# A hybrid decoder step on one Trainium2 core: the squared sums of four norms as two split matmuls in place of one plain fp32 matmul

## The chip, the core and the metric

The kernel runs on one core of a Trainium2 chip (trn2). The metric is the device time of one launch in microseconds, as the median of several executions. The core has five engines with instruction streams of their own: TensorE (PE, matmuls), VectorE (DVE), ScalarE (ACT), GpSimd (POOL) and SyncE (SP, which here only issues DMAs). They wait for each other through semaphores.

## The reference

One decoder layer over 1024 prompt rows and 8 decode rows, all fp32. The parts that matter here are its norms: the LayerNorm behind the convolution, the norm of each head's retention output `o` (the out-norm), and the RMS norms of m and h.

```python
def rms_norm(x, w):
    xf = x.astype(jnp.float32)
    y = xf * lax.rsqrt(jnp.mean(xf * xf, axis=-1, keepdims=True) + EPS)
    return (y * w.astype(jnp.float32)).astype(x.dtype)
...
    a_out = jax.nn.silu(layer_norm(conv, conv_ln_w, conv_ln_b)) @ w_conv_out
...
    S_new, o = retention_scan(qf, kf, vf, ret_state.astype(jnp.float32))
    o = o * lax.rsqrt(jnp.mean(o * o, axis=-1, keepdims=True) + EPS)
    o = o.reshape(B, T, RET_V_WIDTH).astype(xn.dtype)
    b_out = (jax.nn.silu(g) * o) @ w_ret_out

    merged = jax.nn.sigmoid(gate_a) * a_out + jax.nn.sigmoid(gate_b) * b_out
    return merged @ w_o, new_buf, S_new
...
    m, new_buf, S_new = mixer(rms_norm(x, n_mix_pre), conv_buf, ret_state, pos, w_in, w_dw, b_dw,
                              conv_ln_w, conv_ln_b, w_conv_out, w_ret_out, w_o)
    h = x + rms_norm(m, n_mix_post)
    f = jnp.square(jax.nn.relu(rms_norm(h, n_ffn_pre) @ w_up)) @ w_down
    return h + rms_norm(f, n_ffn_post), new_buf, S_new
```

## The kernel before

All activations are held transposed: channels on the 128 partitions, the T = 1032 rows along the free dimension. So the sum over channels that a norm needs is a sum over partitions. VectorE first adds the squares of the channel tiles into one tile, and TensorE then multiplies it by an all-ones 128x128 matrix `ones`; each partition of the result holds the sum. That matmul is plain fp32.

All large products are fp32 by splitting: an operand is a high part (rounded to fp32r by a copy) and a low part (the fp32 value less the high part, again fp32r), and a product is three fp32r matmuls, high by high, high by low and low by high. ScalarE makes the high part of a weight tile, GpSimd the low part, in a ring of three places. Where matrices are large the kernel uses a scheme of seven products for a 2x2 block of tiles: the input projection is 20 units `v` of 7 steps `j`, written (v,j); a step is one product of 24 matmuls of 258 columns. Its results are evicted from PSUM by ScalarE and VectorE in fixed steps; an eviction named e6 or e5 (VectorE, after steps 4 and 5) frees a bank that TensorE needs at step 6, or at step 0 of the next unit. The FFN has 14 up and 16 down units of the same kind.

Between the steps of a unit stands other work, by a schedule written out by hand: after product (v,j) each engine's code calls its `unit_turn(v, j)`, and tables give the turn `x = 7 (v - 13) + j` (and `y = 7 (v - 9) + j`) at which a part is placed. The norms are placed by `NORM_SQUARE` (ScalarE squares 2x344 elements), `NORM_SUM` (VectorE adds the halves), `NORM_STAT` (TensorE's sum, and the root of it on ScalarE: Ln, then Exp) and `NORM_SCALE` (VectorE multiplies, `head_norm`). ScalarE comes to turn j when product j is done; VectorE runs its turns 1 to 4 between the evictions of steps 1 and 4.

The sums by `ones` are:
- three of the first norm at the start (`x_stat`, 344 columns) and the last norm (`f_ones`)
- four of LayerNorm (`ln_stat`, 2x258 columns), for mean and variance of each half of the rows
- twelve of the out-norm (`out_stat`, 344 columns): six of head pair 0 in units 15 to 19, six of head pair 1 (p = 1) in the groups of 36 matmuls behind the units (`b_part`, the first product by `w_ret_out`), after sub-tiles 3, 5, 7, 9, 12 and 14 (`turns_`)
- three of the norm after `w_o` (`mix_stat`, 344 columns)
- two of h (`h_stat`, 2x258 columns) in up unit 9

In pair 1 VectorE also multiplies the finished groups by their gate (`product_gate(e)`), whose end releases on GpSimd an addition `product_add(e)`, and it works the decode rows of the retention.

Of the kernel before, what the change touches and what calls it, by code (L numbers as in the profile page):

```python
# [27 lines left out]
P = 128  # L28
# [26 lines left out]
HT = T // 2  # L55
# [35 lines left out]
X_RET = 13  # L91
RET_A = {1: 0, 3: 1, 6: 2, 8: 3, 11: 4, 13: 5, 16: 6, 18: 7}
# [27 lines left out]
def build(nc, xT, wseq, vecs, wdwT, cacheT, s_in, rope, mask_d, ident_d,  # L120
# [8 lines left out]
    with ExitStack() as ctx:  # L129
# [95 lines left out]
        ones, _ = place("ones", [P, P])  # L225
        vec, _ = place("vec", [P, NVEC])
# [51 lines left out]
        hist_ld = sem("hist_ld")  # L278
# [35 lines left out]
        xs_sc = sem("xs_sc")  # L314
        xs_sum = sem("xs_sum")
        xs_hi = sem("xs_hi")
        xs_lo = sem("xs_lo")
        xw_hi = sem("xw_hi")
        xw_lo = sem("xw_lo")
# [29 lines left out]
        on_ad = sem("on_ad")  # L349
        on_st = sem("on_st")  # L350
# [62 lines left out]
        R_X, R_LN, R_ON, R_M, R_F = 0, CHUNKS, CHUNKS + 2, CHUNKS + 14, 2 * CHUNKS + 14  # L413
        E_WOB = done(S_WOB - 1)
# [185 lines left out]
        def _(sp):  # L600
# [11 lines left out]
            sp.dma_start(hist[:], cacheT).then_inc(hist_ld, 16)  # L612
# [4 lines left out]
            def unit_weights(v):  # L617
# [16 lines left out]
                sp.wait_ge(xw_lo, STEPS * (v - 1) + 6)  # L634
# [124 lines left out]
            for v in range(NV):  # L759
                d = v - UPV  # L760
                p, g = d % 4, d // 4
                if v + 1 < NV:
                    n = OFF + S_FAST + 4 * (v + 1)
                    sp.wait_ge(s_op, 4 * v + 3)
                    sp.wait_ge(q_lo, STEPS * v + 1)
                    sp.dma_start(raw[:, 0, :], wseq[n]).then_inc(raw_ld[0], 16)
                    sp.wait_ge(s_op, 4 * v + 4)
                    sp.wait_ge(q_lo, STEPS * v + 2)
                    sp.dma_start(raw[:, 1, :], wseq[n + 1]).then_inc(raw_ld[1], 16)
                    sp.wait_ge(q_lo, STEPS * v + 4)  # L770
                    sp.dma_start(raw[:, 2, :], wseq[n + 2]).then_inc(raw_ld[2], 16)
                    sp.wait_ge(q_lo, STEPS * v + 5)
# [66 lines left out]
        def _(pool):  # L839
# [85 lines left out]
            def unit_low(v, k):  # L925
# [4 lines left out]
                pool.wait_ge(xw_hi, q + 1)  # L930
                pool.tensor_tensor(lo, src, hi.bitcast(F32), ALU.subtract).then_inc(xw_lo, 1)  # L931
# [58 lines left out]
            def low(v, i):  # L990
# [4 lines left out]
                pool.wait_ge(q_hi, q + 1)  # L995
                pool.tensor_tensor(lo, src, hi.bitcast(F32), ALU.subtract).then_inc(q_lo, 1)  # L996
# [18 lines left out]
        def _(pe):  # L1015
# [208 lines left out]
            def unit_product(v, k):  # L1224
# [18 lines left out]
            def unit_turn(v, j):  # L1243
# [124 lines left out]
            def mix_stat(c):  # L1368

                pe.wait_ge(wo_sum, 6 + 4 * (c + 1))  # L1370
# [4 lines left out]
                pe.matmul(ps[:, 6 + c % 2, 0:CH], ones[:], gbuf[:, 3, c * CH:(c + 1) * CH],  # L1375
                          start=True, stop=True).then_inc(m_st, 1)
# [79 lines left out]
            def product(v, i, between=None):  # L1456
# [67 lines left out]
        def _(act):  # L1524
# [53 lines left out]
            def x_gain(k):  # L1578

                act.activation(x_in[:, k, :], x_in[:, k, :], ACT.Copy, scale=vec[:, V_PRE + k:V_PRE + k + 1]  # L1580
                               ).then_inc(xs_sc, 1)

            def x_operand_hi(i):

                if i == 5:
                    act.wait_ge(mm, done(15))
                    act.activation(xn_h[:, 0:QK, HALVES[1]], sx_5[:], ACT.Copy).then_inc(xs_hi, 1)
# [5 lines left out]
                act.activation(sx_h[:, i - 2], src, ACT.Copy).then_inc(xs_hi, 1)  # L1593
# [41 lines left out]
            def unit_high(v, k):  # L1635
# [14 lines left out]
                act.activation(XRINGS[q % RING][0], src, ACT.Copy).then_inc(xw_hi, 1)  # L1650
# [1503 lines left out]
```

## Time and profile before

| | us |
|---|---|
| median of 3 runs | 1497.67 |
| lowest and highest | 1497.33, 1498.96 |
| span of the profiled execution, first to last instruction | 1495.6 |
| TensorE matmuls busy | 1475.2 (99%) |
| VectorE, GpSimd, ScalarE busy | 1001.0, 842.0, 635.4 |

The profile is of one execution. Its span is 2.1 us below the median of the runs. TensorE's granted clock is 2.4 GHz throughout (0.997 of full speed in the mean). In the rows below, a row of a timeline is: start, duration, engine, line, operation, output <- inputs, shape, count, and in brackets the idle time before it and who ended it. Matmuls are pipelined, and the duration of one covers its way through the array, so that rows overlap; consecutive matmuls of one kind and line are merged (x2, x4).

### The profile page before, as it was taken

To read this page: it belongs to the slowest core of one execution; us is meant where nothing else is said; L and a number is where in the kernel's file an instruction comes from. 1 tells how busy PE (TensorE), PEld (TensorE's weight loads), DVE (VectorE), ACT (ScalarE), POOL (GpSimd) and SP (SyncE) were. 2 spreads that over 40 slices of the span, in tenths; PEclk is the share of its full clock that TensorE was granted. 3 is DMA by queue.
4 is the path that set the end of the run, shared out by engine and by line. 5 is a ranking of instruction groups with operands and counts; after the bars stand their busy time and mean duration, and the time that the engine had idled before them with its cause. 6 is when DMAs were issued, how large, how long until landed. Compare 5 with 4: busy or idle time off the path is not lost.

```text
span 1495.6 us, 28307 instructions
## 1 busy us (share of the span) xinstructions
PE 1475.2 (99%) x11336; PEld 1455.2 (97%) x11336; DVE 1001.0 (67%) x1251; ACT 635.4 (42%) x929; POOL 842.0 (56%) x571
## 2 busy tenths in 40 slices
PE   8999999999999999999999999999999999999996
PEld 5999999999999999999999999999999999999995
DVE  7999888856545724576715876766657765574847
ACT  5533444344544541131213855556556332332333
POOL 3377776777545653257565445555555655554555
PEclk9999999999999999999999999999999999999998
DMA  6013333322356258621421144566759575454634
GB/s 217 22 42 94 114 114 113 113 80 65 112 176 205 75 200 296 219 80 50 149 78 50 29 149 171 199 237 219 253 193 326 203 285 189 142 208 156 227 107 170
DMA packets 110091, 229.13 MB, mean 153 GB/s; under 512 B 8960, under 2 KB 20992, under 8 KB 108304
## 3 DMA queue, kind: packets, MB, share of 16 engines
q1 hardware_dynamic: 95296, 204.30, 39.7%
q10 hardware_dynamic: 14672, 23.09, 4.6%
q8 instruction: 89, 1.46, 0.4%
q14 instruction: 34, 0.28, 0.1%
HBM read 154.41 MB, written 72.95 MB: 152 GB/s over the span
## 4 chain that ended last, share of the span: by engine, by line
PE 96%; POOL 1%; DMA 1%; ACT 1%; issue 1%; DVE 0%; POOLq 0%; SPq 0%; DVEq 0%; ACTq 0%
PE ps L1476 40%; PE ps L1237 26%; PE ps L1026 16%; PE ps L1402 3%; PE ps L1389 3%; PE ps L1074 2%; PE ps L1164 1%; PE ps L1169 1%; PE ps L1180 1%; PE ps L1166 1%; DMA cva_h<-conv_scratch 1%; PE ps L1147 0%; PE ps L1152 0%; PE ps L1194 0%; POOL w_l L931 0%
## 5 line engine op out<-in xcount | busy, mean ns | idle before, releaser
L1476 PE MATMUL ps<-tx_h,w_h 128*128 128x258 f32 x960 | 271.5, 283 | 0.0
L1476 PE MATMUL ps<-tx_l,w_h 128*128 128x258 f32 x960 | 271.3, 283 | 0.0
L1476 PE MATMUL ps<-tx_h,w_l 128*128 128x258 f32 x960 | 271.1, 282 | 0.0
L996 POOL TENSOR_TENSOR w_l<-raw,w_h 128x512 fp32r<-128x512 f32 x120 | 185.6, 1551 | 147.6 <-ACT w_h L2033 147.1
L1476 PE MATMUL ps<-fx_l,w_h 128*128 128x258 f32 x720 | 203.7, 283 | 0.0
L1476 PE MATMUL ps<-fx_h,w_h 128*128 128x258 f32 x720 | 203.6, 283 | 0.0
L1476 PE MATMUL ps<-fx_h,w_l 128*128 128x258 f32 x720 | 203.4, 282 | 0.0
L1476 PEld LDWEIGHTS ps<-tx_h,w_h 128*128 128x128 f32 x960 | 181.4, 189 | 0.1
L1476 PEld LDWEIGHTS ps<-tx_l,w_h 128*128 128x128 f32 x960 | 181.4, 189 | 0.1
L1476 PEld LDWEIGHTS ps<-tx_h,w_l 128*128 128x128 f32 x960 | 181.2, 189 | 0.0
L2328 DVE SCALAR_TENSOR_TENSOR ps<-u_ext,wdw,ps 128x512 f32<-128x512 f32 x232 | 155.2, 749 | 0.0
L2033 ACT ACTIVATE w_h<-raw 128x512 fp32r<-128x512 f32 x120 | 75.7, 631 | 186.8 <-PE ps L1476 179.7
L996 POOL TENSOR_TENSOR w_l<-sum_y,w_h 128x512 fp32r<-128x512 f32 x60 | 91.9, 1532 | 110.2 <-ACT w_h L2033 110.2
L1476 PEld LDWEIGHTS ps<-fx_h,w_h 128*128 128x128 f32 x720 | 136.2, 189 | 0.0
L1476 PEld LDWEIGHTS ps<-fx_l,w_h 128*128 128x128 f32 x720 | 136.0, 189 | 0.0
L1476 PEld LDWEIGHTS ps<-fx_h,w_l 128*128 128x128 f32 x720 | 135.9, 189 | 0.0
L1237 PE MATMUL ps<-xn_h,w_h 128*128 128x258 f32 x416 | 119.6, 287 | 0.0
L1237 PE MATMUL ps<-xn_l,w_h 128*128 128x258 f32 x416 | 117.5, 282 | 0.0
L1237 PE MATMUL ps<-xn_h,w_l 128*128 128x258 f32 x416 | 117.4, 282 | 0.0
L2884 DVE TENSOR_TENSOR fac<-ps,fac 128x516 f32<-128x516 f32 x79 | 54.6, 691 | 83.3 <-PE ps L1476 83.3
L931 POOL TENSOR_TENSOR w_l<-raw,w_h 128x512 fp32r<-128x512 f32 x54 | 76.6, 1418 | 55.2 <-ACT w_h L1650 55.1
L850 POOL TENSOR_TENSOR w_h<-raw,zero 128x512 fp32r<-128x512 f32 x36 | 42.0, 1167 | 108.8 <-PE ps L1026 50.2
(386 smaller groups left out, 4305.4 us busy)
## 6 DMA issues: line engine op xcount, KB each, us to landing
raw<-wseq_dram SPq DMA_DIRECT2D x260, 256.0 KB, 3.1
quad_scratch<-quad_h SPq DMA_DIRECT2D x16, 774.0 KB, 3.5
tx_h<-quad_scratch SPq DMA_DIRECT2D x12, 1032.0 KB, 10.4
tx_l<-hidden_scratch SPq DMA_DIRECT2D x12, 1032.0 KB, 12.8
gate_scratch<-gst SPq DMA_DIRECT2D x10, 1032.0 KB, 5.0
hidden_scratch<-hq_g SPq DMA_DIRECT2D x8, 1032.0 KB, 7.0
hidden_scratch<-stg_b SPq DMA_DIRECT2D x6, 1032.0 KB, 6.9
hq_g<-hidden_scratch SPq DMA_DIRECT2D x6, 1032.0 KB, 13.1
```

Of the source, the lines that this page charges most:

```text
L850: pool.tensor_tensor(hi, raw[:, s, :], zero[:, 0:1].broadcast_to([P, SLOT]), ALU.add).then_inc(w_hi, 1)
L931: pool.tensor_tensor(lo, src, hi.bitcast(F32), ALU.subtract).then_inc(xw_lo, 1)
L996: pool.tensor_tensor(lo, src, hi.bitcast(F32), ALU.subtract).then_inc(q_lo, 1)
L1026: out = pe.matmul(pch(g, c), w[a][:, place_, sub * P:(sub + 1) * P], xs[b][:, k, c * CH:(c + 1) * CH], start=(first and n == 0), stop=(las ...
L1074: out = pe.matmul(pch(G_U + t, c), wp[:, 2 * half + t, sub * P:(sub + 1) * P], x_in[:, k, c * CH:(c + 1) * CH], start=(k == 0), stop=(k == ...
L1237: out = pe.matmul(ps[:, 2 * n + s, 0:HC], XRINGS[q % RING][wa][:, kk * P:(kk + 1) * P], x_operand(i, xb, kk, s), start=(i < 3 and kk == 0 ...
L1389: out = pe.matmul(pch(g, m), (wo_h, wo_l)[a][:, slot, sub * P:(sub + 1) * P], MG[b][:, k, c * CH:(c + 1) * CH], start=(k == 0 and n == 0), ...
L1402: out = pe.matmul(pch(g, c), DIRECT_W[slot][a][:, (k % SLOT_TILES) * P:(k % SLOT_TILES + 1) * P], FX[b][:, k, c * CH:(c + 1) * CH], start= ...
L1476: out = pe.matmul(ps[:, 2 * n + s, 0:HC], RINGS[q % RING][wa][:, kk * P:(kk + 1) * P], OPS[x][xb][:, QK * kh + kk, at_:at_ + HC], start=(i ...
L2033: act.activation(RINGS[q % RING][0], src, ACT.Copy).then_inc(q_hi, 1)
L2328: out = dve.scalar_tensor_tensor(dst, u_, w_, bank, ALU.mult, ALU.add)
L2884: dve.tensor_tensor(dst, pair(n), dst, ALU.add).then_inc(ev_d, 1)
```

## The change

Twenty sums change; the other edits give semaphores of like use one name (`xw_hi` and `q_hi` become `sw_hi`, and so on), which moves nothing. `ones_r` is `ones` rounded to fp32r. For LayerNorm, out-norm, h and the first two chunks of the mix norm, ScalarE copies the sum tile into a high part, VectorE subtracts it for a low part, and TensorE multiplies both by `ones_r`, added in PSUM. In the diff `norm_high` and `ln_high` are ScalarE's copies, `square_low` and `ln_low` VectorE's subtractions. Some of the turns are moved by one, and `h_stat` goes from up unit 9 to 10.

```diff
-NORM_SQUARE = {20: 0, 24: 1, 28: 2, 32: 3, 39: 4, 42: 5}
-NORM_SUM = {21: 0, 26: 1, 30: 2, 33: 3, 40: 4, 43: 5}
-NORM_STAT = {23: 0, 27: 1, 31: 2, 34: 3, 41: 4, 44: 5}
-NORM_SCALE = {26: 0, 29: 1, 33: 2, 35: 3, 42: 4, 45: 5}
+NORM_SQUARE = {20: 0, 24: 1, 28: 2, 32: 3, 39: 4, 43: 5}
+NORM_SUM = {21: 0, 25: 1, 29: 2, 33: 3, 40: 4, 44: 5}
+NORM_SPLIT = {22: 0, 26: 1, 30: 2, 34: 3, 41: 4, 45: 5}
+NORM_STAT = {23: 0, 27: 1, 31: 2, 35: 3, 42: 4, 46: 5}
+NORM_SCALE = {26: 0, 29: 1, 33: 2, 36: 3, 43: 4, 47: 5}
...
-                    out = pe.matmul(ps[:, 6 + s, 0:HC], ones[:], u_ext[:, 0, at_:at_ + HC], start=True, stop=True)
+                    pe.matmul(ps[:, 6 + s, 0:HC], ones_r[:], u_hi_[:, at_:at_ + HC], start=True, stop=False)
+                    out = pe.matmul(ps[:, 6 + s, 0:HC], ones_r[:], u_lo_[:, at_:at_ + HC], start=False, stop=True)
...
-                pe.wait_ge(on_ad, 6 * p + i + 1)
+                pe.wait_ge(st_lo, S_ON + 6 * p + i + 1)
...
-                pe.matmul(ps[:, 6 + i % 2, 0:CH], ones[:], osq[p * (i % 2)][:, 0:CH],
-                          start=True, stop=True).then_inc(on_st, 1)
+                pe.matmul(ps[:, 6 + i % 2, 0:CH], ones_r[:], osq_h[p * (i % 2)][:], start=True, stop=False)
+                pe.matmul(ps[:, 6 + i % 2, 0:CH], ones_r[:], osq_l[p * (i % 2)][:], start=False, stop=True
+                          ).then_inc(on_st, 1)
...
-                if y == 4:
+                if y == 5:
                     taps_done()
-                    pe.wait_ge(ln_sum, 3)
+                    pe.wait_ge(one_r, 1)
+                    pe.wait_ge(st_lo, S_LN + 1)
                     ln_stat(0)
...
-                if y == 18:
+                if y == 19:
                     pe.wait_ge(ln_xc, 8)
-                    pe.wait_ge(ln_sum, 6)
+                    pe.wait_ge(st_lo, S_LN + 2)
                     ln_stat(0)
-                if y == 22:
+                if y == 23:
...
+            def norm_high(p, i):
+
+                b = p * (i % 2)
+                act.wait_ge(on_ad, 6 * p + i + 1)
+                act.activation(osq_h[b][:], osq[b][:, 0:CH], ACT.Copy).then_inc(st_hi, 1)
...
+            def square_low(p, i):
+
+                b = p * (i % 2)
+                dve.wait_ge(st_hi, S_ON + 6 * p + i + 1)
+                dve.tensor_tensor(osq_l[b][:], osq[b][:, 0:CH], osq_h[b][:].bitcast(F32), ALU.subtract
+                                  ).then_inc(st_lo, 1)
...
+                if y in (3, 18):
+                    ln_low(y // 18)
...
             norm_square(1, 1)
+            norm_high(1, 0)
+            norm_high(1, 1)
             for i in range(2 * CHUNKS):
                 norm_root(1, i)
...
                 if i + 2 < 2 * CHUNKS:
                     norm_square(1, i + 2)
+                    norm_high(1, i + 2)
...
             wob_out(0, 1)
+            mix_high(0)
...
             wob_out(1, 1)
+            mix_high(1)
...
-                    if v == 9 and i in (2, 5):
+                    if v == 10 and i in (2, 5):
                         h_stat(i // 3)
```

VectorE's stream of pair 1, from the first two adds to the gate of group 1. Before (L2505 is the add of the squares, L2512 `head_norm`, L2637 `product_gate`, L2500 the copy of a decode output):

```order
L2505 TENSOR_TENSOR osq_144<-osq_144 128x344
L2505 TENSOR_TENSOR osq_145<-osq_145 128x344
L2512 TENSOR_TENSOR v_95<-v_95,ps 128x2x344
L2484 COPY qd_b<-qk_94 128x2
...
L2505 TENSOR_TENSOR osq_144<-osq_144 128x344
L2500 COPY v_95<-ps 128x4
L2637 TENSOR_TENSOR bop_b<-ps,gb 128x1032
L2512 TENSOR_TENSOR v_95<-v_95,ps 128x2x344
L2505 TENSOR_TENSOR osq_145<-osq_145 128x344
L2512 TENSOR_TENSOR v_95<-v_95,ps 128x2x344
L2500 COPY v_95<-ps 128x4
L2637 TENSOR_TENSOR bop_b<-ps,gb 128x1032
```

The same stream in the changed kernel (L2564 the add, L2571 the new low part, L2578 `head_norm`, L2707 `product_gate`):

```order
L2564 TENSOR_TENSOR osq_155<-osq_155 128x344
L2564 TENSOR_TENSOR osq_156<-osq_156 128x344
L2571 TENSOR_TENSOR osq_l_151<-osq_155,osq_h_153 128x344
L2571 TENSOR_TENSOR osq_l_152<-osq_156,osq_h_154 128x344
L2578 TENSOR_TENSOR v_95<-v_95,ps 128x2x344
...
L2707 TENSOR_TENSOR bop_b<-ps,gb 128x1032
L2571 TENSOR_TENSOR osq_l_151<-osq_155,osq_h_153 128x344
L2578 TENSOR_TENSOR v_95<-v_95,ps 128x2x344
L2564 TENSOR_TENSOR osq_156<-osq_156 128x344
L2578 TENSOR_TENSOR v_95<-v_95,ps 128x2x344
L2571 TENSOR_TENSOR osq_l_152<-osq_156,osq_h_154 128x344
```

Low part 0 stands behind add 1, low part 2 behind the gate, and low part 3 behind `head_norm` 2.

ScalarE's stream at the same place in the changed kernel (L1775 Square, L1782 the new high part, L1547 and L1549 the root); before, it was the same without the rows of L1782:

```order
L1775 ACTIVATE osq_156<-v_95 128x688
L1782 ACTIVATE osq_h_153<-osq_155 128x344
L1782 ACTIVATE osq_h_154<-osq_156 128x344
L1547 ACTIVATE ps<-ps,eps_b 128x344
L1549 ACTIVATE ps<-ps 128x344
L1757 DMA rets_dram<-s_dec 128x2x256
L1775 ACTIVATE osq_155<-v_95 128x688
L1782 ACTIVATE osq_h_153<-osq_155 128x344
L1547 ACTIVATE ps<-ps,eps_b 128x344
L1549 ACTIVATE ps<-ps 128x344
L1775 ACTIVATE osq_156<-v_95 128x688
L1782 ACTIVATE osq_h_154<-osq_156 128x344
```

High part 0 stands behind Square 1, and each later root behind the high part of the sum after it.

VectorE around step 5 of unit 16 in the changed kernel (L2675 the eviction of step 4, L2571 the low part of sum 1 of pair 0, L2578 `head_norm`, L2680 the eviction of step 5); before, the add stood at the place of the low part:

```order
L2564 TENSOR_TENSOR osq_155<-osq_155 128x344
L2675 TENSOR_TENSOR v_95<-ps,v_95 128x516
L2571 TENSOR_TENSOR osq_l_151<-osq_155,osq_h_153 128x344
L2559 COPY v_105<-ps 128x4
L2578 TENSOR_TENSOR v_105<-v_105,ps 128x2x344
L2680 TENSOR_TENSOR v_95<-ps,v_95 128x516
```

The add went one turn ahead, and the low part came in front of `head_norm` and the eviction.

## Rows read from the trace of the kernel before

**Rows 1.** The page: span, and busy time of each engine.

```profile
span 1495.6 us, 28307 instructions
PE 1475.2 (99%) x11336; PEld 1455.2 (97%) x11336; DVE 1001.0 (67%) x1251; ACT 635.4 (42%) x929; POOL 842.0 (56%) x571
```

**Rows 2.** Waits of TensorE, the longest: us in total, times, longest.

```profile
PE ps L1074 <- DVE wp L2286: 5.8, 1, 5.8
```

**Rows 3.** Instructions that read `ones`, the out-norm: durations in ns, first and last start.

```profile
L1194 PE MATMUL ps<-osq,ones x24: 450/452/455, 477.0 to 662.1; 128*128 128x344 f32 x24
```

**Rows 4.** Timeline of TensorE around a mix sum and a LayerNorm sum.

```profile
800.41 0.32 PE L1389 MATMUL ps<-mg_h,wo_l 128*128 128x344 f32 x1
800.57 0.74 PE L1375 MATMUL ps<-gbuf,ones 128*128 128x344 f32 x2
...
801.30 0.32 PE L1389 MATMUL ps<-mg_l,wo_h 128*128 128x344 f32 x1
...
302.94 0.28 PE L1237 MATMUL ps<-xn_h,wx_l 128*128 128x258 f32 x1
303.06 1.03 PE L1131 MATMUL ps<-u_ext,ones 128*128 128x258 f32 x4
...
304.05 0.28 PE L1237 MATMUL ps<-sx_l,w_h 128*128 128x258 f32 x1
```

**Rows 5.** Timeline of TensorE, the out-norm sums 0, 2, 3, 4 and 5 of pair 1.

```profile
641.61 0.74 PE L1194 MATMUL ps<-osq,ones 128*128 128x344 f32 x2
...
649.30 0.74 PE L1194 MATMUL ps<-osq,ones 128*128 128x344 f32 x2
...
653.59 0.74 PE L1194 MATMUL ps<-osq,ones 128*128 128x344 f32 x2
...
658.41 0.74 PE L1194 MATMUL ps<-osq,ones 128*128 128x344 f32 x2
...
661.82 0.74 PE L1194 MATMUL ps<-osq,ones 128*128 128x344 f32 x2
```

**Rows 6.** Timeline of ScalarE at pair 1: Square 1, Ln of root 0, Square 2.

```profile
641.74 0.78 ACT L1750 ACTIVATE osq<-v 128x688 f32<-128x688 f32 x1 [3.60 <-issue]
642.42 0.50 ACT L1527 ACTIVATE ps<-ps,eps_b 128x344 f32<-128x344 f32 x1
...
647.66 0.78 ACT L1750 ACTIVATE osq<-v 128x688 f32<-128x688 f32 x1 [4.27 <-DVE s_dec L2494]
```

**Rows 7.** Timeline of VectorE at pair 1: add 1, gate 0, `head_norm` 1, add 3.

```profile
642.54 0.52 DVE L2505 TENSOR_TENSOR osq<-osq 128x344 f32<-128x344 f32 x1 [2.29 <-ACT osq L1750]
...
648.98 1.22 DVE L2637 TENSOR_TENSOR bop_b<-ps,gb 128x1032 f32<-128x1032 f32 x1
650.12 0.86 DVE L2512 TENSOR_TENSOR v<-v,ps 128x688 f32<-128x688 f32 x1
650.90 2.17 DVE L2505 TENSOR_TENSOR osq<-osq 128x344 f32<-128x344 f32 x1
```

**Rows 8.** Timeline of GpSimd at pair 1: `product_add(0)`.

```profile
650.28 2.41 POOL L951 TENSOR_TENSOR ma<-ma,bop_b 128x1032 f32<-128x1032 f32 x1 [4.59 <-DVE bop_b L2637]
```

**Rows 9.** Timelines of ScalarE, VectorE, GpSimd and TensorE at LayerNorm sum 2.

```profile
340.63 1.06 ACT L1670 ACTIVATE u_ext<-conv 128x1032 f32<-128x1032 f32 x1
...
346.28 0.67 ACT L1527 ACTIVATE ps<-ps,eps_b 128x516 f32<-128x516 f32 x1
...
345.41 0.70 DVE L2605 TENSOR_TENSOR v<-ps,v 128x516 f32<-128x516 f32 x1 [1.52 <-PE ps L1237]
...
346.45 1.29 POOL L931 TENSOR_TENSOR w_l<-raw,w_h 128x512 fp32r<-128x512 f32 x1
...
345.21 1.03 PE L1131 MATMUL ps<-u_ext,ones 128*128 128x258 f32 x4
```

**Rows 10.** Timelines of VectorE and GpSimd after product (16,5).

```profile
487.38 0.70 DVE L2610 TENSOR_TENSOR v<-ps,v 128x516 f32<-128x516 f32 x1 [1.54 <-PE ps L1237]
...
488.09 1.74 POOL L931 TENSOR_TENSOR w_l<-raw,w_h 128x512 fp32r<-128x512 f32 x1 [0.70 <-ACT w_h L1650]
```

More of the change, by code:

```diff
@@ L225, in build @@
         ones, _ = place("ones", [P, P])
+        ones_r, _ = place("ones_r", [P, P], F32R)
         vec, _ = place("vec", [P, NVEC])
@@ L244, in build @@
         sum_y, _ = place("sum_y", [P, SLOT], F32, a_ST + 4 * SLOT)
+        hms_h, _ = place("hms_h", [P, T], F32R, a_C0 + 8 * T)
+        hms_l, _ = place("hms_l", [P, T], F32R, a_ST + 8 * SLOT)
+        mst_h, _ = place("mst_h", [P, 2, CH], F32R, a_G)
+        mst_l, _ = place("mst_l", [P, 2, CH], F32R, a_G + 12 * T)
         hms, _ = place("hms", [P, T], F32, a_ST + 8 * SLOT)
@@ L248, in build @@
         rtab = [place(f"rtab{c}", [P, 2, HC], F32, a_Q + (8 * HC + 16) * c if c < 3 else a_PB)[0] for c in range(4)]
+        u_lo_, _ = place("u_lo_", [P, T], F32R, a_C1)
+        u_hi_, _ = place("u_hi_", [P, T], F32R, a_C1 + 4 * UW + 8)
+        osq_l = [place(f"osq_l{i}", [P, CH], F32R, (a_KT, a_PB)[i])[0] for i in range(2)]
+        osq_h = [place(f"osq_h{i}", [P, CH], F32R, (a_KT, a_PB)[i] + 4 * CH)[0] for i in range(2)]
         osq = [place("osq0", [P, 2 * CH], F32, a_KT)[0], place("osq1", [P, 2 * CH], F32, a_PB)[0]]
@@ L313, in build @@
         cvl_st = sem("cvl_st")
-        xs_sc = sem("xs_sc")
+        g_sc = sem("g_sc")
         xs_sum = sem("xs_sum")
[L316 to L319, printed above, removed]
+        op_hi = sem("op_hi")
+        op_lo = sem("op_lo")
+        sw_hi = sem("sw_hi")
+        sw_lo = sem("sw_lo")
         xw_op = sem("xw_op")
@@ L349, in build @@
         on_ad = sem("on_ad")
+        st_hi = sem("st_hi")
+        st_lo = sem("st_lo")
+        one_r = sem("one_r")
         on_st = sem("on_st")
@@ L1368, in mix_stat @@
             def mix_stat(c):
-                pe.wait_ge(wo_sum, 6 + 4 * (c + 1))
+                if c < 2:
+                    pe.wait_ge(st_lo, S_M + c + 1)
+                else:
+                    pe.wait_ge(wo_sum, 6 + 4 * (c + 1))
                 if c == 0:
@@ L1374, in mix_stat @@
                     pe.wait_ge(m_sc, 2)
-                pe.matmul(ps[:, 6 + c % 2, 0:CH], ones[:], gbuf[:, 3, c * CH:(c + 1) * CH],
-                          start=True, stop=True).then_inc(m_st, 1)
+                out = ps[:, 6 + c % 2, 0:CH]
+                if c < 2:
+                    pe.matmul(out, ones_r[:], mst_h[:, c, :], start=True, stop=False)
+                    pe.matmul(out, ones_r[:], mst_l[:, c, :], start=False, stop=True).then_inc(m_st, 1)
+                else:
+                    pe.matmul(out, ones[:], gbuf[:, 3, c * CH:(c + 1) * CH], start=True, stop=True).then_inc(m_st, 1)
             for c in range(CHUNKS):
@@ L1490, in h_stat @@
                 for s in range(2):
-                    out = pe.matmul(ps[:, 6 + s, 0:HC], ones[:], hms[:, t * HT + s * HC:t * HT + (s + 1) * HC],
-                                    start=True, stop=True)
+                    at_ = t * HT + s * HC
+                    pe.matmul(ps[:, 6 + s, 0:HC], ones_r[:], hms_h[:, at_:at_ + HC], start=True, stop=False)
+                    out = pe.matmul(ps[:, 6 + s, 0:HC], ones_r[:], hms_l[:, at_:at_ + HC], start=False, stop=True)
                 out.then_inc(x_st, 1)
@@ L2018, in _ @@
                 act.wait_ge(t_f, min(i, 4))
-                quad_hi(i, mix[:, KHALVES[kh], HALVES[th]]).then_inc(t_hi, 1)
+                quad_hi(i, mix[:, KHALVES[kh], HALVES[th]]).then_inc(op_hi, 1)
             def high(v, i):
@@ L2107, in up_unit @@
                 if v == 9:
+                    h_high()
+                if v == 10:
                     h_root(0)
@@ L2229, in _ @@
             dve.memset(ones[:], 1.0).then_inc(c_init, 1)
+            dve.wait_ge(c_init, 1)
+            dve.tensor_copy(ones_r[:], ones[:]).then_inc(one_r, 1)
             dve.memset(eps_b[:], EPS).then_inc(c_init, 1)
@@ L2642, in _ @@
             square_sum(1, 1)
+            square_low(1, 0)
+            square_low(1, 1)
             head_norm(1, 0)
@@ L2734, in _ @@
             wob_sum(1, 1)
+            mix_low(1)
             fx_lo_part(0)
@@ L2778, in _ @@
                 kh, th = X_OF[i][1:]
-                dve.wait_ge(t_hi, i - 1)
+                dve.wait_ge(op_hi, 4 + i - 1)
                 dve.wait_ge(t_f, 4)
-                quad_lo(dve, i, mix[:, KHALVES[kh], HALVES[th]]).then_inc(t_lo, 1)
+                quad_lo(dve, i, mix[:, KHALVES[kh], HALVES[th]]).then_inc(op_lo, 1)
             def hidden_lo(u):
```

120 lines of the change are left out of this document (73 added, 47 removed).

## Prediction

> **What bounds the kernel now.** I read the page of the profile first: matmuls are busy for 99% of the span [rows 1]. The waits of TensorE come next: the only long one is at the start, 5.8 us for the first scaled weights [rows 2]. So the other engines are always ahead, and two things can change the time: what TensorE itself issues, and a wait that becomes longer than the lead its releaser has. Third, I read the instructions that read `ones`: the 12 out-norm sums are 24 records [rows 3], since a plain fp32 matmul leaves two. A record's duration is no price here, as matmuls overlap; the distance between starts is.
>
> **What the change takes from TensorE.** At 344 columns the sum starts at 800.57 and the second matmul behind it at 801.30. Split matmuls of 344 columns start 0.16 us apart (800.41 to 800.57), so one plain sum occupies 0.73 - 0.16 = 0.57 us. Of 2x258 columns it occupies 304.05 - 303.06 - 0.12 = 0.87 us, where split matmuls start 0.12 us apart [rows 4]. The new sums are two split matmuls of the same columns: 0.32 us and 4 x 0.12 = 0.48 us. Saved: 0.25 us in each of 14 sums (12 out-norms, 2 of mix) and 0.39 us in each of 6 (4 of LayerNorm, 2 of h): 3.5 + 2.3 = 5.8 us. Nothing covers this, TensorE has no idle time around it. The start, the third mix sum and the end keep the plain form. The cast of `ones` falls before TensorE's first wait ends.
>
> **What it adds.** Each sum gets a copy on ScalarE (0.5 us at 344 columns, as the Ln of that width [rows 6]; 1.06 us at 1032, as the Square in [rows 9]) and a subtraction on VectorE (0.52 us at 344, as the add ahead of it, and 1.2 us at 1032, as `product_gate` [rows 7]). These cost nothing where the lead is longer. Where the schedule gave the sums one turn more (a turn is one product, 24 split matmuls of 0.12 us: 2.9 us), the sums themselves are in time: I followed each sum of pair 0, and its low part is ready 0.3 to 2 us ahead. The h sums sit in a unit where both engines are half idle, and both mix sums come 3 us and more after their low parts. Three places are left.
>
> **Place 1: out-norms of pair 1.** Here nothing was moved on TensorE, and four links were put in the chain.
> Sum 0: TensorE comes to it at 641.61 [rows 5]. ScalarE now does Square 1 (641.74 to 642.52), then high 0 (to 642.95) [rows 6]; VectorE does add 1 (642.54 to 643.06) [rows 7], then low 0, to 643.5. TensorE waits 1.9 us. Behind its wait stand all the matmuls of the group.
> Sum 1: no wait, low 1 is done at 644.1.
> Sum 2: root 0 (Ln and Exp, 0.5 us each) starts 0.5 us after sum 0, at 644.0 instead of 642.42, and through `head_norm` 0 (0.86) and the decode work behind it Square 2 moves from 647.66 [rows 6] to 647.9, as the slack between them takes up most of it. Add 2 ends at 649.2, `product_gate(0)` (1.22 us) at 650.4, low 2 at 650.8. TensorE arrives at 649.30 + 1.9 - 2 x 0.25 = 650.7: a wait of 0.15 us.
> Sum 3: before, add 3 began at 650.90 and took 2.17 us instead of 0.52 [rows 7], because GpSimd had its `product_add` of 2.41 us running since 650.28 [rows 8]. It still does, since `product_gate(0)` releases that one: at 650.8, behind low 2, it starts for 2.3 us, and add 3 ends near 653.4. Now high 3 (0.5), root 2 (1.0), `head_norm` 2 (0.86) and low 3 (0.45) follow in series, since ScalarE has root 2 queued behind high 3, and VectorE has `head_norm` 2 queued ahead of low 3. That is 656.2. TensorE arrives 4.29 - 0.25 us after sum 2 [rows 5], at 654.9, and waits 1.4 us.
> Sums 4 and 5: TensorE takes 4.82 and 3.41 us to them, less 0.25; the same series needs about 4.7 and 3.3: waits of some 0.2 us each.
> Together 3.9 us. Bounds: sum 0 alone, 1.9, if the rest keeps its lead; 5.0 if low 4 falls under a GpSimd instruction of 1.0 to 1.3 us too. I take 3.9. Downstream nothing gives it back, as TensorE waits for nothing there.
>
> What decides sum 3 is the collision with GpSimd. The Trainium skill (SBUF — State Buffer, Who interferes with whom) says that a VectorE instruction with two SBUF inputs and a GpSimd instruction that reads SBUF exclude each other, the first to issue holding the port to its end; the trace agrees, with 2.17 us instead of 0.52. By that rule the added subtractions, all of two SBUF inputs, are themselves exposed, and the sum stands as above; with free ports add 3 would end at 652.0, sum 3 would wait for nothing, and 1.4 us would go from the total. The rule speaks against this change.
>
> **Place 2: unit (16,5).** Low part 1 of pair 0 stands on VectorE ahead of `head_norm(0,0)` and of the last eviction of unit 16. ScalarE makes high part 1 only when product (16,5) is done and the next weight copy is out. Before, the eviction of (16,5) began at 487.38 [rows 10], as soon as that product was done (near 487.2). Now: high 1 at 487.9 to 488.4; GpSimd's low weight part starts at 488.09 [rows 10] and lasts 1.3 us (as in [rows 9]; its 1.74 there came from a VectorE instruction under way); low 1 is at 489.4 to 489.8, `head_norm` to 490.7 (0.86), the eviction (0.70) to 491.3. TensorE wants that bank at 487.2 + 2.9 + 0.3 = 490.4, after product (16,6) and sum 1. It waits 0.9 us; if low 1 gets ahead of GpSimd, 0.1. I take 0.9.
>
> **Place 3: second LayerNorm sum.** The low part stands ahead of the eviction of product (11,4), which ran at 345.41. ScalarE's slot for the high part is where root 0 began, 346.28, so it ends at 347.3; GpSimd's instruction runs to 347.74; the low part ends at 348.9 [rows 9]. TensorE reaches the moved sum at 345.21 + 2.88 = 348.1 and waits 0.8 us; the eviction behind it (0.70 us, to 349.6) adds 0.1, since (11,6) needs it at 348.9 + 0.5. In all 0.9 us; if GpSimd's were not in the way, 0.5.
>
> **The sum.** -5.8 + 3.9 + 0.9 + 0.9 = -0.1 us, against the span of 1495.6 us. The median is 2.1 us above that span; this remainder stays. 1497.67 - 0.1: I say 1497.5. A measurement of this kernel tells about 0.2% (3.0 us) from no change.
>
> **Rivals.**
> Leads hold (0.20): only the wait at sum 0 (1.9 us) and a remnant of 0.5 us come. For it: I place additions to 0.3 us, and several of my waits are 0.2. Against: sum 3's series of 2.8 us follows an add that was ready only 0.5 us ahead (653.07 to 653.59). It gives 1497.7 - 5.8 + 2.4 = 1494.3; with no waits at all, 1491.9.
> GpSimd wins the port (0.12), slower: at pair 1, low 2 and add 4 come straight behind a `product_gate`, whose end also releases a `product_add`. Before, VectorE's next began at 650.12 and GpSimd's at 650.28 [rows 7, 8], so VectorE was ahead by 0.16 us. Should the semaphores of the new low part cost it this 0.16 us, it waits out 2.4 us, and so at the second gate: 1497.6 + 4.8 = 1502.4. From 0.16 us on this decides.
> The pairs are no cheaper (0.04): should `ones_r` matmuls need 0.57 us, the gain is gone: 1497.7 + 5.7 = 1503.4. Against it stand the kernel's split matmuls at 0.16 and 0.12 us [rows 4].
> The forecast, gain and waits within 3 us of each other, has 0.64.
>
> **Range.** The forecast's own range is 1495.0 to 1500.5: place 1 between 2.0 and 5.0, place 2 between 0.1 and 1.2, place 3 between 0.5 and 1.3. For 8 in 10 I add the edge of the first rival and some of the second: 1494.0 to 1501.0. Faster 0.21, same 0.62, slower 0.17: the first rival and a tail; the forecast; the last two and a tail.
>
> **What would show it.** TensorE's waits list the sums of pair 1 with about 2 us and 1.4 us, behind VectorE's low part; the record at (17,0) waits for the eviction; the moved LayerNorm sum waits for its low part. Starts around each new sum are 0.32 and 0.48 us apart. If the waits of pair 1 after the first are missing, the first rival holds; if the low part there takes over 2 us, the second. I am wrong as well if an eviction that I left out (of units 17 to 19) becomes late.

## The result, and the profile after

The changed kernel takes 1500.9 us (median of 12 runs, 1500.6 to 1501.9) against 1497.43 of the kernel before (12 runs, 1497.2 to 1499.0). The ratio is 1.0023, with a 95% interval of 1.0015 to 1.0031: slower by 3.5 us, where I had said no change. It stands inside my range by 0.1 us.

The page of the changed kernel, which answers to [rows 1]:

```profile
span 1498.7 us, 28344 instructions
PE 1472.5 (98%) x11336; PEld 1453.9 (97%) x11336; DVE 1010.0 (67%) x1269; ACT 644.0 (43%) x946; POOL 846.4 (56%) x571
```

The span grew by 3.1 us (before 1495.6), and TensorE is busy for 2.7 us less. The gain is there, and waits have outgrown it. TensorE's six longest waits, which answer to [rows 2] (releaser, us in total, times, longest):

```profile
PE ps L1083 <- DVE wp L2341: 5.8, 1, 5.8
PE ps L1204 <- DVE osq_l L2571: 2.7, 3, 1.5
PE ps L1248 <- DVE v L2680: 0.8, 1, 0.8
PE ps L1140 <- DVE u_lo__149 L2488: 0.7, 1, 0.7
PE ps L1147 <- DVE conv L2502: 0.7, 1, 0.7
PE ps L1248 <- DVE v L2559: 0.6, 1, 0.6
```

Below the wait at the start, all are new. The sums of pair 1 (L1204), the bank at (17,0) (L2680) and the second LayerNorm sum (L1140, the first of the two variance sums) were forecast. The transpose of decode values at (13,0) (L1147) and the copy of a decode output (L2559) were not.

For the size of each I laid the matmuls of both traces side by side, one by one, and read by how much the start of the same matmul had moved. What a sum saved is added back, so the table shows the cost of a wait. It is mostly some 0.2 us more than the idle time of a record, as the first matmul behind an idle time is slower too (0.27 us to the next start instead of 0.16 behind sum 0):

| place | forecast, us | measured, us |
|---|---|---|
| 20 sums, saved | -5.8 | -6.0 |
| pair 1, sum 0 | 1.9 | 1.8 |
| pair 1, the matmuls between sum 0 and sum 1 | 0 | 1.5 |
| pair 1, sums 2, 3, 4, 5 | 0.15, 1.4, 0.2, 0.2 | 0, 1.0, 0, 0.7 |
| place 2, (17,0) | 0.9 | 1.0 |
| place 3, second LayerNorm sum | 0.9 | 1.1 |
| (16,3), bank of a decode output | 0 | 0.8 |
| (13,0), transpose of decode values | 0 | 0.7 |
| sums 4 and 5 of pair 0, less what came back near 557 us; FFN; before the first LayerNorm sum | 0 | 0.1; 0.3; 0.1 |
| sum | -0.1 | +3.1 |

The second row of pair 1 is no wait. A timeline of TensorE in the changed kernel, where [rows 5] showed sum 0 at 641.61:

```profile
643.86 0.42 PE L1204 MATMUL ps<-osq_h,ones_r 128*128 128x344 f32 x1 [1.52 <-DVE osq_l L2571]
644.13 0.32 PE L1205 MATMUL ps<-osq_l,ones_r 128*128 128x344 f32 x1
644.28 0.95 PE L1190 MATMUL ps<-qd_b,s_dec 128*128 128x1 f32 x8
645.09 0.93 PE L1035 MATMUL ps<-ro_h,w_h 128*128 128x344 f32 x3
645.82 1.06 PE L1035 MATMUL ps<-ro_l,w_h 128*128 128x344 f32 x3
646.68 1.06 PE L1035 MATMUL ps<-ro_h,w_l 128*128 128x344 f32 x3
...
649.07 0.64 PE L1035 MATMUL ps<-ro_h,w_l 128*128 128x344 f32 x3
649.54 0.32 PE L1204 MATMUL ps<-osq_h,ones_r 128*128 128x344 f32 x1
```

Three matmuls take 0.86 us from 645.82 to 646.68, and 0.47 from 649.07 to 649.54. Some twelve starts are 0.29 us apart instead of 0.16, which is 1.55 us in all. The reason stands in the busy time by stretch (stretch, its length, PE busy with its instructions, granted clock, DMA share, GB/s):

```profile
643.00:645.25 2.25, 1.39 (x11) 1.00 0.61 188
645.50:648.75 3.25, 3.25 (x13) 0.50 0.01 3
649.00:651.00 2.00, 2.00 (x15) 1.00 0.78 251
```

The granted clock is 0.50 of full speed, that is 1.2 GHz, from 645.4 to 648.8, behind an idle time of 1.5 us; in the kernel before it was 1.00 throughout this stretch. The Trainium skill (TensorE: Matmul & The Clock Gate, The HAM clock gate) has the clock at one of two levels, by how busy TensorE has been. The trace has only these two levels, 0.50 and 1.00; what busyness brings it down is not shown here.

VectorE in the same stretch, beside [rows 7] of before:

```profile
643.30 1.16 DVE L2571 TENSOR_TENSOR osq_l<-osq,osq_h 128x344 fp32r<-128x344 f32 x2
645.51 0.87 DVE L2578 TENSOR_TENSOR v<-v,ps 128x688 f32<-128x688 f32 x1 [1.06 <-ACT ps L1549]
646.30 0.16 DVE L2543 COPY qd_b<-qk 128x2 f32<-128x2 f32 x1
646.37 1.63 DVE L2548 TENSOR_SCALAR v_bc<-v_bc,qk 128x256 f32<-128x256 f32 x2
648.03 0.76 DVE L2553 SCALAR_TENSOR_TENSOR s_dec<-s_dec,v_bc 128x256 f32<-128x256 f32 x2
650.07 0.52 DVE L2564 TENSOR_TENSOR osq<-osq 128x344 f32<-128x344 f32 x1 [1.27 <-ACT osq L1775]
...
650.57 1.22 DVE L2707 TENSOR_TENSOR bop_b<-ps,gb 128x1032 f32<-128x1032 f32 x1
651.71 0.51 DVE L2571 TENSOR_TENSOR osq_l<-osq,osq_h 128x344 fp32r<-128x344 f32 x1
```

Low 2 (L2571 at 651.71) ends at 652.2, and sum 2 starts at 652.68. Without the slow clock TensorE would have been there 1.55 us sooner, at 651.1, and would have waited 1.1 us for low 2. So the two costs do not simply add, and experiments must say what each is worth. I had forecast low 2 for 650.8. The whole stretch stands 0.6 us later than before by what was lost ahead of it. And the two multiplies of `v_bc` (L2548), which took 0.61 us before, took 1.63, because GpSimd's split of the next weights, released by TensorE behind sum 0, now lies beside them:

```profile
645.38 1.04 POOL L859 TENSOR_TENSOR w_h<-raw,zero 128x512 fp32r<-128x512 f32 x1 [5.84 <-PE ps L1190]
646.50 1.35 POOL L862 TENSOR_TENSOR w_l<-raw,w_h 128x512 fp32r<-128x512 f32 x1
```

In the kernel before, the same split had ended at 645.69, just ahead of the multiplies:

```profile
644.39 1.30 POOL L853 TENSOR_TENSOR w_l<-raw,w_h 128x512 fp32r<-128x512 f32 x1
...
645.79 0.61 DVE L2489 TENSOR_SCALAR v_bc<-v_bc,qk 128x256 f32<-128x256 f32 x2 [1.41 <-DMA v_bc<-v_sample_scratch]
```

### The profile page after: what moved, and what is told of

Read it like the earlier page. It is cut to its first block, busy times and chain, and to the rows that moved or that the text cites. A ratio compares the mean times of both kernels' runs of the same rounds, so it can differ in the third digit from the quotient of the medians.

```text
span 1498.7 us, 28344 instructions
## 1 busy us (share of the span) xinstructions
PE 1472.5 (98%) x11336; PEld 1453.9 (97%) x11336; DVE 1010.0 (67%) x1269; ACT 644.0 (43%) x946; POOL 846.4 (56%) x571
## 3 DMA queue, kind: packets, MB, share of 16 engines
q8 instruction: 89, 1.46, 0.4%
## 4 chain that ended last, share of the span: by engine, by line
PE 91%; DVE 4%; ACT 2%; issue 1%; POOL 1%; DMA 1%; SPq 0%; ACTq 0%; POOLq 0%; DVEq 0%
PE ps L1495 40%; PE ps L1248 24%; PE ps L1035 14%; PE ps L1421 3%; PE ps L1408 3%; PE ps L1174 1%; PE ps L1179 1%; PE ps L1176 1%; PE ps L1190 1%; DMA x_in<-xT_dram 1%; DVE x_in L2319 0%; PE ps L1157 0%; PE ps L1162 0%; POOL w_l L940 0%; DMA v_bc<-v_sample_scratch 0%
```

## The experiments

All times are compared with 1497.4 to 1497.5 us, the median of the kernel before on the same chip in each group of runs.

**1. Pair 1: high 0 and low 0 first.** On ScalarE and VectorE:

```diff
 norm_square(1, 0)
 decode_store(1, DEC - 2)
+norm_high(1, 0)
 decode_load(1, DEC - 1)
 value_load(1, DEC - 1)
 norm_square(1, 1)
-norm_high(1, 0)
 norm_high(1, 1)
...
 square_sum(1, 0)
+square_low(1, 0)
 square_sum(1, 1)
-square_low(1, 0)
 square_low(1, 1)
```

> The changed kernel with high part 0 of pair 1 made ahead of the two DMA issues and Square 1 on ScalarE, and low part 0 ahead of add 1 on VectorE. Add 0 ends at 640.9, so low part 0 should be ready near 642.0, when TensorE comes to sum 0 (642.2). In the changed kernel TensorE idled 1.5 us there, and from 645.4 to 648.8 its granted clock was 0.50: 18 matmuls behind sum 0 started 0.29 us apart instead of 0.16. Theory (the idle time brought the clock down): both go, 1.7 us of wait and 1.7 us of slow clock, less some 0.4 us that sums 2 and 3 then wait longer; about 3.0 us less than the changed kernel, 1497.9 us, and a clock of 1.00 from 642 to 650. Rival (the slow stretch has a cause of its own, such as the decode work on VectorE and GpSimd's weight split that run in it): only the wait goes, 1.7 us less, 1499.2 us, and the 18 matmuls still start 0.29 us apart.

Measured: 1499.44 us (1499.1 to 1500.2), 1.5 below the changed kernel. That is near the rival's 1499.2, but not for the rival's reason. In the profiled execution the clock stays at 1.00 through pair 1, so that part of the theory stood. But TensorE's timeline has this:

```profile
641.93 0.43 PE L1204 MATMUL ps<-osq_h,ones_r 128*128 128x344 f32 x1
...
646.09 0.32 PE L1204 MATMUL ps<-osq_h,ones_r 128*128 128x344 f32 x1
...
650.84 0.42 PE L1204 MATMUL ps<-osq_h,ones_r 128*128 128x344 f32 x1 [1.46 <-DVE osq_l L2571]
...
656.22 0.43 PE L1204 MATMUL ps<-osq_h,ones_r 128*128 128x344 f32 x1 [1.08 <-DVE osq_l L2571]
```

Sums 0 and 1 come at once, and sums 2 and 3 wait instead. ScalarE shows why low 2 is late:

```profile
644.28 0.44 ACT L1549 ACTIVATE ps<-ps 128x344 f32<-128x344 f32 x1
647.38 0.38 ACTq L1757 DMA_DIRECT2D rets_dram<-s_dec  x1
647.82 0.78 ACT L1775 ACTIVATE osq<-v 128x688 f32<-128x688 f32 x1 [3.09 <-DVE s_dec L2553]
649.18 0.49 ACT L1782 ACTIVATE osq_h<-osq 128x344 fp32r<-128x344 f32 x1 [0.58 <-DVE osq L2564]
```

From 644.7 to 647.8 it stands idle: Square 2 is queued behind the decode store, which waits for VectorE's decode state. So pair 1 has a chain of its own (decode state, Square 2, add 2, `product_gate(0)`, low 2), and a gain at sum 0 runs into it.

**2. The same, with high 0 behind the two DMA issues.** `norm_high(1, 0)` stands directly ahead of `norm_square(1, 1)`.

> The changed kernel with high part 0 of pair 1 made ahead of Square 1 but behind the two DMA issues on ScalarE, and low part 0 ahead of add 1. High part 0 then begins near 642.0 and low part 0 ends near 643.0: sum 0 comes 0.8 to 0.9 us sooner, and TensorE idles some 0.6 us instead of 1.5. Theory (the clock falls only after an idle time longer than some bound between 1.0 and 1.5 us): the slow stretch goes whole, so 0.9 + 1.7 = 2.6 us less than the changed kernel, 1498.3 us. Rival (each wait costs its own length, and the slow stretch has another cause): 0.9 us less, 1500.0 us.

Measured: 1500.11 us; in the profiled execution idle times of 0.70, 1.34, 1.06 and 0.40 us at sums 0, 2, 3 and 5, and a clock of 1.00 there. The time is near the rival's 1500.0, but not for its reason: the slow stretch did go, and the chain behind sum 0 took the gain.

**3 and 4. The kernel before, with sum 0 held back.** All sums are plain; the second version adds a copy on VectorE to hold it longer.

```diff
-pe.wait_ge(on_ad, 6 * p + i + 1)
+pe.wait_ge(on_ad, 6 * p + i + 1 + (p == 1 and i == 0))
```

> The kernel before, all sums plain, with sum 0 of pair 1 waiting for add 1 as well as for its own add 0. Add 1 ended at 643.06, and TensorE came to the sum at 641.61, so it waits 1.5 us, with about 1.3 us idle in the records. Theory (idle time brings the clock down): above the kernel before by 1.5 us, and by 1.7 us more if 1.3 us are enough: 1500.7 us; 1499.0 if they are not. Rival (the slow stretch comes from the split sums or the work around them): 1499.0 us, at a clock of 1.00 throughout.

> The kernel before, with sum 0 of pair 1 held until VectorE has done add 1 and one copy of 344 elements behind it: TensorE waits about 1.9 us, 1.7 of them idle. Theory (idle time brings the clock down): 1.9 us of wait and 1.7 us of slow clock over the kernel before, 1501.1 us, with a granted clock of 0.50 for some 3.5 us that begins 1 to 2 us behind the wait. Rival (the slow stretch comes from the split sums or the work around them): 1.9 us, 1499.4, and no fall of the clock.

Measured: 1499.78 us (1498.8 to 1501.3) and 1500.82 (1499.5 to 1503.0). The profiled executions idled for 1.35 and 1.76 us and show no fall of the clock; these two had 1499.56 and 1499.46 us:

```profile
643.38 0.82 PE L1196 MATMUL ps<-osq,ones 128*128 128x344 f32 x2 [1.76 <-DVE osq L2507]
```

But the ten runs of the second spread over 3.5 us, where the kernel before spreads over 1.1, and they order by their mean clock: four at 0.996 of full speed with 1499.5 to 1500.0 us, three at 0.995 with 1500.7 to 1501.6, three at 0.994 with 1502.5 to 1503.0. So do the ten of the first version: six at 0.996 and 0.997 with 1498.8 to 1500.0 us, four at 0.995 with 1500.3 to 1501.3. A stretch as in the changed kernel, half the clock for 3.4 us, is 0.001 of the mean. So a held sum seems to bring slow stretches in some executions and none in others.

The mean clock needs one caution. In every trace it is 0.50 at the end as well (in the kernel before from 1486.2 us, 4.8 us behind the last matmul), so the clock before is 2.4 GHz throughout only up to there, and this end alone moves the mean by up to 0.001. Yet the split is clean: none of the runs of the kernel before in the groups of the experiments, and none of experiments 5, 9, 10 and 11, which have no long idle time in pair 1, lies below 0.996. The changed kernel has 9 of 12 there, and each of the other experiments at least 3 of 10.

Over all profiled kernels, 11 idle times of TensorE in pair 1 were of 1.0 to 1.9 us. Behind four of them (1.52, 0.98, 1.44 and 1.93 us) came a stretch of 3.4 us at 0.50, in which the matmuls fell back by 1.55 us each time (1.7, in my expectations, is half of 3.4); behind seven (1.46, 1.08, 1.34, 1.06, 1.35, 1.76 and 1.47 us) none. Nor did one come behind four idle times of 0.9 to 1.2 us near 38 us. The length alone does not decide it.

**5. Pair 1 plain.** The changed kernel with the high and low parts of pair 1 left out, and its sums over `ones`.

> The changed kernel with the six out-norm sums of pair 1 plain again, no high or low parts for them, all other split sums kept. Aligned matmul by matmul, the changed kernel falls back by 3.4 us against the kernel before within pair 1. Theory (pair 1 costs 3.4 us net, and all else together comes to nothing): 3.4 us less than the changed kernel, 1497.5 us, the same as before. Rival (the time lost in units 11 to 19 is the larger part): less than 2 us, above 1499.

Measured: 1497.30 us, ratio 1.000 (0.999 to 1.001). The theory holds: pair 1 is the whole loss, and the 14 other sums came to nothing.

**6 and 7. The other waits.** Sums 0 and 1 of pair 0 plain (`NORM_SPLIT` without them, `NORM_SUM` as before); and the variance sums of LayerNorm plain, at turns 18 and 22, with `ln_scale(0)` at 20.

> The changed kernel with out-norm sums 0 and 1 of pair 0 plain again, at the turns of the kernel before. This undoes the two waits that I read there: at product (16,3) for the copy of a decode output (net 0.5 us), and at (17,0) for the last eviction of unit 16 (net 0.76 us). Theory (both come from low parts 0 and 1 on VectorE): 1.25 us less than the changed kernel, 1499.65 us, both waits gone. Rival (they come from TensorE being ahead by what it saved earlier, whatever VectorE does): the waits stay, and the time is 0.5 us longer for the two plain sums, 1501.4 us.

> The changed kernel with the two variance sums of LayerNorm plain again and all their turns as before. It gives up 0.8 us of TensorE's saving. Theory (moving sum and root by a turn is what made the low part late, and two turns on made the scale late for which the decode transpose at unit 13 waits): both waits, 1.0 and 0.7 us, go, so 1.0 us less than the changed kernel, 1499.9 us. Rival (VectorE reaches the scale at its own pace, and the wait is there because TensorE is ahead): the wait at the transpose stays in part, and the time is within 0.3 us of the changed kernel.

Measured: 1499.98 and 1499.68 us, 0.9 and 1.2 below the changed kernel. The waits at (16,3) and (17,0) are gone in the one, those at the LayerNorm sum and the transpose in the other; at the entry of pair 1 the same matmuls stand 0.9 and 1.1 us earlier than in the changed kernel. (Counted from just ahead of each edit it is 1.4 and 0.9 us, as two executions differ by some tenths already there.) Both theories hold: these waits go with the splits. How (16,3) came to wait is seen on VectorE in the changed kernel:

```profile
475.60 1.33 DVE L2571 TENSOR_TENSOR osq_l<-osq,osq_h 128x344 fp32r<-128x344 f32 x1 [0.35 <-ACT osq_h L1782]
476.85 0.68 DVE L2468 TENSOR_TENSOR qk<-v,rtab 128x516 f32<-128x516 f32 x1
477.45 0.68 DVE L2469 TENSOR_TENSOR v<-v,rtab 128x516 f32<-128x516 f32 x1
478.06 0.15 DVE L2559 COPY v<-ps 128x4 f32<-128x4 f32 x1
```

Low 0 is in time for its sum (477.23). Behind it stand two multiplies of the rotary embedding and then a copy of 0.15 us, for whose bank TensorE waits at 478.36. Low 0 took 1.33 us instead of 0.52 as GpSimd was at work.

The transpose waits for `ln_scale(1)`, whose own turn was not moved. It came 0.3 us late (at 373.56, before 373.23), while TensorE stood 0.4 us earlier. Ahead of it VectorE has a join of the rotary embedding, and this fell under a GpSimd instruction; the same join in the kernel before took half the time:

```profile
370.08 1.30 POOL L915 TENSOR_TENSOR wx_x<-raw 128x512 f32<-128x512 f32 x1
...
370.35 1.58 DVE L2476 TENSOR_TENSOR q0s<-q0s,rtmp 128x516 f32<-128x516 f32 x1
```

```profile
370.76 0.84 DVE L2422 TENSOR_TENSOR q0s<-q0s,rtmp 128x516 f32<-128x516 f32 x1
```

GpSimd's instruction ran 0.3 us later than before, at the end of a chain of weight splits that a ScalarE copy releases (365.43, before 365.13); the moved root 1 now stands ahead of that copy. This chain is read from the rows; the experiment shows only that the wait goes with the moved turns.

**8. Pair 1 in another order.** High 0 and low 0 as in 1; Square 2 and high 2 ahead of the decode store, add 2 and low 2 ahead of the decode state, low 3 ahead of `product_gate(0)`, root 3 ahead of Square 4.

> The changed kernel with the work of pair 1 put in another order on ScalarE and VectorE, TensorE's program untouched: high and low part 0 as in the first experiment; Square 2 and high 2 ahead of the decode store; add 2 and low 2 ahead of the decode state; add 3 and low 3 ahead of product_gate(0), so that GpSimd's addition is not yet running; root 3 ahead of Square 4; lows ahead of the head_norm that waits for a root. Theory (what sets pair 1's pace is the order of these streams: sum 2 waited 1.5 us in the first experiment because Square 2 stood behind the decode store and low 2 behind the gate): no wait over 0.3 us at any of the six sums, and TensorE keeps their saving of 1.5 us; 3.4 + 1.5 = 4.9 us less than the changed kernel, 1496.0 us, 1.4 us below the kernel before. Rival (the pace is set by what comes by DMA, the decode values that arrive near 645.8): as the first experiment, 1499.4 us, since the wait goes to the next sum.

Measured: 1499.64 us. No sum waited over 0.2 us, as the theory said, and the time is still the rival's. I had made a new wait myself:

```profile
649.96 0.32 PE L1205 MATMUL ps<-osq_l,ones_r 128*128 128x344 f32 x1
650.11 0.95 PE L1190 MATMUL ps<-qd_b,s_dec 128*128 128x1 f32 x8
652.99 0.74 PE L1035 MATMUL ps<-ro_h,w_h 128*128 128x344 f32 x3 [1.93 <-DVE bop_b L2715]
```

`product_gate(0)` (L2715) frees the bank of group 2 and had gone behind low 3. After this idle time too the clock fell, from 654.0 to 657.4.

**9. The same with the gates in time.** VectorE's stream of pair 1:

```python
head_norm(1, 0)
square_sum(1, 2)
square_low(1, 2)
decode_state(1, DEC - 1)
square_sum(1, 3)
product_gate(0)
square_low(1, 3)
head_norm(1, 1)
product_gate(1)
head_norm(1, 2)
square_sum(1, 4)
square_low(1, 4)
head_norm(1, 3)
square_sum(1, 5)
square_low(1, 5)
```

> The reordered pair 1 once more, with the gates in their place. In the experiment before, the six sums waited 0.2 us in all, but product_gate(0) had gone behind low 3 and ended at 652.9, and TensorE waited 1.9 us for its bank (from 651.06). Now add 3, then product_gate(0), then low 3, so that the gate ends near 651.1; product_gate(1) ahead of head_norm 2; root 3 behind high 4. Theory (pair 1's waits come from the order of the two streams): no wait over 0.3 us between 640 and 670, TensorE keeps 1.5 us there, and the time is 1496.2 us, 4.7 less than the changed kernel. Rival (something that no order changes, the decode values' DMA or the speed of the chain itself, holds pair 1): another wait of over 1 us comes up, 1499.5 us.

Measured: 1496.06 us, ratio 0.9990 (0.9981 to 0.9999). TensorE has no idle time over 0.1 us between 560 and 750, and 4.84 us of the changed kernel's time are gone, against 4.7 expected.

**10. All mended.** The order of 9 with the plain sums of 6 and 7.

> The order of the kernel above, and with it sums 0 and 1 of pair 0 and the two variance sums of LayerNorm plain at their old turns, as in two experiments before, which took off 1.34 and 1.05 us in the records. Theory (the places are independent, and the rest of the saving is real): 1500.9 - 4.7 - 1.3 - 1.0 = 1493.9 us, 3.6 below the kernel before. Rival (pair 1 waits for a chain that does not begin on TensorE, so that whatever is saved ahead of it is given back there): 1496.2 us, as the kernel above.

Measured: 1493.88 us (1493.6 to 1494.7), ratio 0.9976 (0.9967 to 0.9985): faster than before by 3.6 us. The page and all of TensorE's waits:

```profile
span 1491.7 us, 28338 instructions
PE 1470.2 (99%) x11336; PEld 1452.7 (97%) x11336; DVE 1010.7 (68%) x1266; ACT 642.3 (43%) x943; POOL 843.6 (57%) x571
```

```profile
PE ps L1083 <- DVE wp L2358: 5.7, 1, 5.7
PE ps L1035 <- ACT sgt L1605: 1.0, 1, 1.0
PE ps L1257 <- ACT v L1897: 0.2, 1, 0.2
PE ps L1257 <- POOL w_l L940: 0.2, 1, 0.2
```

The 1.0 us at L1035 is near 38 us and has nothing to do with the sums: in this execution TensorE was 1.3 us ahead of the kernel before at 20 us, and 0.1 us ahead behind the wait.

**11. Split sums only where they were covered.** Pair 1, sums 0 and 1 of pair 0 and the variance sums plain, the order as before.

> Split sums only where no wait was read: the two mean sums of LayerNorm, sums 2 to 5 of pair 0, two of mix, two of h; all of pair 1, sums 0 and 1 of pair 0 and the variance sums plain, in the order of the kernel before. Saved: 2 x 0.39 + 4 x 0.25 + 2 x 0.25 + 2 x 0.39 = 3.1 us, less 0.9 us of waits that stay (0.5 at the first mean sum, 0.2 in unit 19, 0.2 at the operand of the FFN). Theory (the saving of a sum is real wherever its low part is in time): 1497.4 - 2.2 = 1495.2 us. Rival (all saved ahead of pair 1 is given back there, where VectorE and ScalarE set the pace): only mix and h count, 1497.4 - 1.1 = 1496.3 us.

Measured: 1495.04 us, ratio 0.9983 (0.9974 to 0.9992): the theory holds. Of the waits that I had listed as staying, the 0.5 us at the first mean sum is not there: I had misread a plain sum of 0.87 us in the comparison of the traces. Experiments 9 to 11 together rule out that pair 1 gives back what is saved ahead of it, once its order is right. (In experiment 11, with the old order and plain sums, 0.3 of 2.0 us came back at sum 2.)

## Why the prediction was wrong

**The gain was right.** "Saved: 3.5 + 2.3 = 5.8 us" held. The halves of a split sum start 0.16 us apart (649.54 and 649.70), and behind sums that nothing waited for, the same matmuls come 0.25 to 0.28 us (344 columns) and 0.37 to 0.42 us (2x258) earlier, 6.0 us in all. The third rival, that pairs are no cheaper, is out.

**Place 1 was right at sum 0, and two steps behind it failed.** I gave it 3.9 us of waits, and it cost 5.0. Sum 0 (1.9, measured 1.8) and sum 3 (1.4, measured 1.0) were named with their causes. Sum 5 waited 0.7 and not 0.2, as its add took 1.35 us beside a GpSimd instruction.

The first step that failed is the sentence that TensorE "waits 1.9 us. Behind its wait stand all the matmuls of the group": I priced an idle time of 1.5 us at its length, and TensorE ran at half clock for 3.4 us behind it, 1.55 us more. No stretch of the trace before, past the start, had an idle time of this size from which to read a price, but the start had one, of 5.8 us, after which the clock was 1.00; so a bound was missing above.

**The step on sum 2 failed too, though its number came out.** I wrote that Square 2 "moves from 647.66 to 647.9, as the slack between them takes up most of it". It moved to 649.26, by 1.6 us: 0.6 by what was lost ahead of pair 1, and 1.0 because the multiplies of `v_bc` ran beside GpSimd's displaced weight split (1.63 us instead of 0.61). That sum 2 did not wait is luck: the slow clock hid it, as experiment 1 shows, where sum 2 idled for 1.46 us.

So the slow stretch is not the whole answer. It stands in the place of a wait at sum 2 that I had priced at 0.15 us. Experiment 1, in which sum 0 is in time, is only 1.5 us faster than the changed kernel, and not the 3.3 us that both terms at sum 0 had cost. In experiment 6 the clock did not fall behind sum 0 (1.47 us idle); there sum 2 idled for 0.98 us, the clock fell behind that one, and pair 1 came to 5.0 us all the same. And of the changed kernel's 12 runs three have a mean clock of 0.997, with 1500.9 to 1501.4 us, no faster than the other nine. That sum 2 waits in these three is argued, not seen.

**Places 2 and 3 held**: 0.9 forecast for each, 1.0 and 1.1 measured, the waits released by the instructions that I had named; experiments 6 and 7 undo them.

**What I left out cost 2.0 us.** "I followed each sum of pair 0, and its low part is ready 0.3 to 2 us ahead" is a statement on the sums, and nearly all of it is true (only sums 4 and 5 waited, 0.1 and 0.3 us, most of which came back near 557 us). The failed step is what it was used for: that these sums therefore cost nothing. The wait at (16,3), 0.8 us, is for a copy queued behind low 0; the one at (13,0), 0.7 us, is for `ln_scale(1)`. The variance sums and their roots were moved by a turn, TensorE stood 0.4 us earlier and VectorE 0.3 us later, and I did not look for what reads the scaled rows. For place 2 I had asked what stands behind a low part on VectorE, and I did not ask it at most others. In the profiled execution these and the slow clock make the difference from -0.1 to +3.1: 1.5 + 2.0 - 0.3 of the other terms.

**The rivals.** "Leads hold" is out. "GpSimd wins the port" is out as well: behind `product_gate(0)` VectorE's low 2 started first (651.71 against 651.87) and took 0.51 us. I had no rival that put a price on idle time itself.

**What stays open** is why the clock falls behind one idle time and not behind a longer one. Only a single execution of each kernel has a trace; that the spread of experiments 3 and 4 comes from such stretches is argued from the mean clocks, not seen.

## What to carry to other kernels

Work that is put into an engine's stream costs what stands behind it, not only what reads it: for every added instruction, list the next few on its engine and who waits for each, evictions and one-line copies first. On a kernel whose TensorE never idles, a new wait of a microsecond or more may cost more than its length, so bound it from above with a stretch at the lower clock (here 1.55 us); and where another engine's chain is late anyway, as here, ask how much of either would come back. And a late operand is a matter of order before it is one of cost: the same 20 splits went from 3.5 us slower to 1.5 us faster when only pair 1's streams were put in order, and to 3.6 us faster with four sums left plain.

## What the runs showed of the hardware

In pair 1, an idle time of 1.0 to 1.9 us on TensorE was followed in 4 of 11 cases by 3.4 us at a granted clock of 0.50, beginning 1.0 to 2.4 us after work had resumed; the matmuls, 0.29 us apart instead of 0.16, fell back by 1.55 us in each.

A VectorE multiply by a per-partition scalar (`v_bc`, 128x256), with a single large SBUF input, takes 0.35 us. In the changed kernel 4 of 32 took 1.37 to 1.42 us; each had started 0.02 to 0.2 us after a GpSimd instruction and ended 0.15 us after it. I had expected this only of instructions with two large SBUF inputs, such as the add of 2.17 us [rows 7]. The trace before had it already, in 2 of its 32 (1.41 and 1.38 us).
